# First modulation matrix loaded by feature tile, first two dense units with the contraction outside, small loads on SyncE

## What is computed

```python
x = layer_norm(x, emb_ln_g, emb_ln_b)
cs = jax.nn.silu(c)
mod = cs @ w_ada[l] + b_ada[l]                 # [1, 1024] @ [1024, 6144]
sh1, sc1, gt1, sh2, sc2, gt2 = split(mod, 6)
h = x * (1.0 + sc1) + sh1                      # modulation of the 1024 features
p = h @ w_in[l]                                # then gMLP on one part, RWKV-7 mixing on the other
```

## Time and profile before

| | |
|---|---|
| median of three runs | 1488.13 us (1479.65 to 1488.69) |
| profiled execution | 1484.96 us, its span 1483.1 us |
| PE busy | 1392.3 us, 94% of the span |
| DVE, ACT, POOL busy | 44%, 38%, 33% |
| chain that ended last | PE 82%, DVE 9%, ACT 3%, issue 2%, DMA 2%, POOL 2% |
| PE busy, first two of 40 slices of 37 us | 4 and 8 tenths |

### The profile page before, as it was taken

How to read it: one execution, slowest core, us unless ns; L and a number is a source line. 1 busy time by engine, 2 the same in 40 slices (tenths; PEclk the granted TensorE clock), 3 DMA queues, 4 the chain that set the end, 5 groups by cost and what they waited for, 6 DMA issues and landing times.

```text
span 1483.1 us, 22792 instructions
## 1 busy us (share of the span) xinstructions
PE 1392.3 (94%) x9482; PEld 1146.5 (77%) x9482; DVE 648.0 (44%) x1160; ACT 560.2 (38%) x836; POOL 495.9 (33%) x139
## 2 busy tenths in 40 slices
PE   4899999889899999999997999999999999998998
PEld 1687866775788888878887778888788888887886
DVE  2655677363555333330027524687345444452001
ACT  2435455243432322221214444555454343433122
POOL 1333233014333443433432231112233344443434
PEclk9899999998999999999998998999999999999999
DMA  9662265001312223233212620101221323222221
GB/s 355 188 152 82 86 229 201 31 3 58 113 58 103 96 85 114 85 108 117 88 60 69 249 81 5 58 30 58 72 86 57 114 85 108 92 88 97 96 75 57
DMA packets 24741, 147.93 MB, mean 100 GB/s; under 512 B 2716, under 2 KB 3868, under 8 KB 9024
## 3 DMA queue, kind: packets, MB, share of 16 engines
q1 hardware_dynamic: 19296, 130.96, 24.1%
q10 hardware_dynamic: 5344, 15.51, 3.9%
HBM read 141.74 MB, written 4.72 MB: 99 GB/s over the span
## 4 chain that ended last, share of the span: by engine, by line
PE 82%; DVE 9%; ACT 3%; issue 2%; DMA 2%; POOL 2%; SPq 0%; ACTq 0%; DVEq 0%; POOLq 0%
PE bank L2009 23%; PE bank L2011 22%; PE bank L2010 22%; PE bank L2268 5%; PE bank L1161 2%; DMA raw<-in_weights 2%; POOL weight_lo L1272 2%; PE bank L2175 1%; PE bank L1152 1%; ACT weight_hi L1317 1%; PE bank L1143 1%; DVE bank L1656 1%; PE bank L1070 1%; DVE xres L1656 1%; PE bank L1139 1%
## 5 line engine op out<-in xcount | busy, mean ns | idle before, releaser
L1272 POOL TENSOR_TENSOR weight_lo<-raw,weight_hi 128x2048 fp32r<-128x2048 f32 x98 | 445.7, 4548 | 838.1 <-ACT weight_hi L1317 838.0
L2009 PE MATMUL bank<-act_hi,weight_hi 128*128 128x512 f32 (+1 forms) x1136 | 436.5, 384 | 22.4 <-DVE act_lo L1653 7.1
L2011 PE MATMUL bank<-act_hi,weight_lo 128*128 128x512 f32 (+1 forms) x1136 | 427.3, 376 | 0.0
L2010 PE MATMUL bank<-act_lo,weight_hi 128*128 128x512 f32 (+1 forms) x1136 | 427.1, 376 | 0.0
L1317 ACT ACTIVATE weight_hi<-raw 128x2048 fp32r<-128x2048 f32 x98 | 185.2, 1891 | 403.1 <-PE bank L2011 394.4
L2009 PEld LDWEIGHTS bank<-act_hi,weight_hi 128*128 128x128 f32 x1136 | 218.2, 192 | 63.0 <-issue 15.8
L2011 PEld LDWEIGHTS bank<-act_hi,weight_lo 128*128 128x128 f32 x1136 | 217.7, 192 | 38.9
L2010 PEld LDWEIGHTS bank<-act_lo,weight_hi 128*128 128x128 f32 x1136 | 218.2, 192 | 35.0 <-issue 0.2
L2009 PE MATMUL bank<-weight_hi,hid_hi 128*128 128x512 f32 x352 | 139.0, 395 | 6.9 <-DVE acc L1656 4.7
L2010 PE MATMUL bank<-weight_lo,hid_hi 128*128 128x512 f32 x352 | 138.8, 394 | 0.0
L2011 PE MATMUL bank<-weight_hi,hid_lo 128*128 128x512 f32 x352 | 138.4, 393 | 0.0
(11 more groups left out here) (361 smaller groups left out, 1720.7 us busy)
## 6 DMA issues: line engine op xcount, KB each, us to landing
raw<-in_weights SPq DMA_DIRECT2D x120, 1024.0 KB, 4.6
w<-in_w ACTq DMA_DIRECT2D x2, 2048.0 KB, 10.4
bias_rows<-grow ACTq DMA_DIRECT2D x1, 2560.0 KB
xres<-in_x SPq DMA_DIRECT2D x4, 512.0 KB, 6.7
strip<-bias_rows ACTq DMA_DIRECT2D x1, 2048.0 KB, 9.0
out<-xres SPq DMA_DIRECT2D x3, 512.0 KB, 2.6
row_a<-in_ln_g ACTq DMA_DIRECT2D x2, 512.0 KB, 3.9
row_b<-in_ln_b ACTq DMA_DIRECT2D x2, 512.0 KB, 4.8
```

The lines of the kernel that those rows point to most:

```text
L1272: pool.tensor_tensor(wlo[i % SPLIT][:, :size], raw[n % RAW][:, :size], whi[i % SPLIT][:, :size], ALU.subtract).then_inc(lo_ready, 1)
L2009: pe.matmul(o, l[0], r[0], start=first, stop=False)
L2010: pe.matmul(o, l[0], r[1], start=False, stop=False)
L2011: return pe.matmul(o, l[1], r[0], start=False, stop=last)
```

## The change

- The first 2048 modulation columns are no longer loaded by row tile but by feature tile: `ada0_b` now holds, for feature tile b, all 1024 rows of its 128 sh1 and 128 sc1 columns. The bytes are the same. PE makes eight matmuls of 256 columns (`ada_block`), four at a time in the four column groups of the array, then two matmuls with one column (`columns_block`) that add up the four partial rows by a vector with ones in rows 0, 32, 64, 96 (`group_rows`).
- Every feature tile now has its own chain: `ada_block`, ACT's `mod_half`, `columns_block`, DVE's `mod_column` (three instructions), ACT's `affine_hi`, DVE's `affine_lo`, and the products with it.
- The unit order is now `lora0`, `ada0_0`, `ada0_1`, `k0`, `ada0_2` to `ada0_7`, `lora1`, `k1`, `r0`. Both `lora0` and `k0` run with k outside, interleaved with the modulation blocks; ACT converts `k0` between `affine_hi(0)` and `affine_hi(1)`. `lora1` is third.
- The fifteen small loads go out on SP, after the loads of `ada0_7`, `k1` and `r0`.

```diff
-    win = [("lora0", ((lora, 256),)), ("lora1", ((lora + 160, 128),))]
-    win += [(f"k{j}", ((base + MIX + 256 * j, 256),)) for j in range(2)]
+    win = [("lora0", ((lora, 256),)), ("k0", ((base + MIX, 256),)), ("lora1", ((lora + 160, 128),)),
+           ("k1", ((base + MIX + 256, 256),))]
...
+    first = [(f"ada0_{k}", "w_ada", 0, KC, ((k * P, P), (DM + k * P, P))) for k in range(KC)]
...
-    units = win[:1] + [(f"ada0_{k}", "w_ada", k * P, 1, ((0, 2 * DM),)) for k in range(KC)] + win[1:] + ada
+    units = win[:1] + first[:2] + win[1:2] + first[2:] + win[2:] + ada
...
+    for k in range(KC):
+        b.add(("h1", k), 4 + k % 2, dve=1, act=1)
+        b.add(("ada0", k), 6 + k % 2, act=1, ada=k + 1)
+        b.add(("cols0", k), 6 + k % 2, dve=1)
...
+            elif UNITS[n][0] == "ada0_7":
+                sp.dma_start(relb[0:N_BUCKETS, :], src["rel_bias_t"]).then_inc(load["rel"], 16)
...
+        def mod_half(k):
+
+            await_full(act, ("ada0", k))
+            a.done(act.activation(acc[:, 256 * (k % 2):256 * (k % 2) + 256], bank(("ada0", k))[:, 0:256], ACT.Copy),
+                   drain(("ada0", k), "act"))
+
+        def affine_hi(k):
+
+            await_drained(act, ("cols0", k), "dve")
+            await_full(act, ("h1", k))
+            a.done(act.activation(act_hi[:, k, :], bank(("h1", k))[:], ACT.Identity, bias=affine[:, 1, k:k + 1],
+                                  scale=affine[:, 0, k:k + 1]), drain(("h1", k), "act"))
+
+        for t in range(2):
+            normalise(0, t, S["xn_ready"])
+        mod_half(0)
+        for t in range(2, TT):
+            normalise(0, t, S["xn_ready"])
+        mod_half(1)
+        affine_hi(0)
+        convert()
+        affine_hi(1)
+        for k in range(2, KC):
+            mod_half(k)
+            affine_hi(k)
...
-            if name != W_IN1[-1]:
+            if name not in ("lora1", W_IN1[-1]):
                 convert()
...
+        def mod_column(k):
+
+            b, sh, sc = bank(("cols0", k)), pc[:, COLS["b_sh1"] + k:COLS["b_sh1"] + k + 1], modc[:, k:k + 1]
+            await_full(dve, ("cols0", k))
+            ts(affine[:, 0, k:k + 1], b[:, 257:258], sc, col("emb_g", k), ALU.add, ALU.mult)
+            ts(affine[:, 1, k:k + 1], b[:, 257:258], sc, col("emb_b", k), ALU.add, ALU.mult)
+            stt(affine[:, 1, k:k + 1], b[:, 256:257], sh, affine[:, 1, k:k + 1], ALU.add, ALU.add, sem=drain(("cols0", k), "dve"))
...
+        d.step(V.memset(group_rows, 0.0))
+        for n in range(4):
+            d.step(V.memset(scalars[ROW * n:ROW * n + 1, 0:1], 1.0), S["rows_ready"])
...
+        def ada_block(b):
+
+            n = UNIT_AT[f"ada0_{b}"]
+            claim(pe, ("ada0", b))
+            raw_ready(pe, n)
+            for k in range(KC):
+                r = slice(ROW * (k % 4), ROW * (k % 4) + ROW)
+                mm = pe.matmul(bank(("ada0", b))[r, 0:256], col("c", k).to_broadcast([P, ROW]),
+                               raw[n % RAW][:, 256 * k:256 * k + 256], start=k < 4, stop=k >= 4)
+            mm.then_inc(ada_used, 1)
...
         pe.wait_ge(S["silu_c"], 1)
-        for i in range(5):
-            ada(i)
+        pe.wait_ge(S["rows_ready"], 4)
+        ada_block(0)
+        columns_block(0)
+        ada_block(1)
         pe.wait_ge(load["consts"], 32)
-        turn_x("h1", (S["xn_ready"], 0), features=range(KC - 1))
-        for i in range(5, KC):
-            ada(i)
-        columns(0)
-        turn_x("h1", (S["xn_ready"], 0), features=range(KC - 1, KC))
...
+        turn_x((0, 1), wait=True)
+        columns_block(1)
+        lora0 = next_unit("lora0")
+        for b in range(2, KC):
+            ada_block(b)
+            first_products("lora0", lora0, b - 2)
+            turn_x((b,))
+            columns_block(b)
+            if b == 4:
+                k0 = next_unit("k0")
+            if b >= 4:
+                first_products("k0", k0, b - 4)
+        first_products("lora0", lora0, KC - 2)
+        first_products("k0", k0, KC - 4)
+        first_products("lora0", lora0, KC - 1)
+        for k in range(KC - 3, KC):
+            first_products("k0", k0, k)
```

More of the change, by code:

```diff
@@ L139 @@
 HALF = SEQ // 2
+W_IN1 = ("lora0", "k0", "lora1", "k1", "r0", "r1", "v0", "v1", "pv0", "pv1", "pu0", "pu1")
 class Order:
@@ L2211, in prep_pe @@
+        for k in range(KC - 3, KC):
+            first_products("k0", k0, k)
+        pe.wait_ge(load["rel"], 32)
+        claim(pe, "bias")
+        fill("bias", pe.matmul(bank("bias")[0:N_HEADS, :], relb[0:N_BUCKETS, :], onehot[0:N_BUCKETS, :], start=True, stop=True))
         def prep_pe(p, part):
@@ L2233, in _ @@
             else:
-                dense_feature(name, 1 if name == "lora1" else 2, stage="h1" if name == W_IN1[0] else None)
-            if name == "lora0":
-                pe.wait_ge(load["rel"], 32)
-                claim(pe, "bias")
-                fill("bias", pe.matmul(bank("bias")[0:N_HEADS, :], relb[0:N_BUCKETS, :], onehot[0:N_BUCKETS, :],
-                                       start=True, stop=True))
+                dense_feature(name, 1 if name == "lora1" else 2)
             if name == "r0":
```

142 lines of the change are left out of this document (62 added, 80 removed).

## The result

The changed kernel took 1474.31 us in the median of 20 runs (1466.09 to 1480.44), the kernel before 1481.99 in 20 runs beside them (1472.63 to 1488.81). The ratio is 0.9938, with a 95% interval of 0.9922 to 0.9954: faster by 0.5 to 0.8%, which still counts as "same". The forecast said 1485.3 us, range 1475 to 1492, and same with a chance of 0.92. The direction and the class came out; the number is 11.0 us off, and 0.7 us outside the range.

A forecast was written before the change was run, and what follows sets the result against it. PE, 82% of the last-ending chain, was taken as the bound, so only its idle or slow stretches count. `r0` moves from 86.1 to 83.3 us, 2.8 gained; from the median 1488.13 that gives 1485.3 us, range 1475 to 1492.

The forecast's parts named there:

- The first two blocks: Head: block 0 starts at 13.93 us, its column matmuls end at 18.4, block 1 runs to 20.4.
- The high and low part of `k0`: Head: eight transposes at 0.16 us, high part done at 24.8 us, POOL's low part at 29.5.
- A new wait on SP: `ada0_4`'s load waits for `k0`'s low part; nothing to move from about 25 to 29.5 us, block 4 at 34.1.
- `act_lo(1)`: DVE subtraction held beside POOL's split of `k0`, ending at about 30 us; hidden by the missing block load.
- PE from 34.1 us: Blocks, products and transposes end `k0` at 62.8 us at full clock, 64.0 with 1.2 us for slow clock.
- What is late next: Ahead of `r0`: tile 1's row pair, held by POOL, delays the low-rank inputs about 1.3 us; `r0` at 83.3 us.
- The shift of `r0`: End of the head: `r0` starts at 83.3 us instead of 86.1, the whole gain of 2.8 us.
- The small loads: Fifteen loads moved from ACT to SP: priced at nothing, as their 4.61 us are covered on either engine.
- Rival 1: Head: no hole in the loads, `r0` at about 78.0 us, gain 8 us, 1480 us; chance 0.14.
- Rival 2: PE at 1.2 GHz from 22 to 62 us: `r0` at 105, 19 us slower, 1507 us; chance 0.04 in full.
- rival 3: Head's seams cost 0.3 us instead of 0.1: `r0` 2 us later, 1490 us; chance 0.25 with partly slow clock.
- My last test: If `r0` starts as forecast but the total moves by over 5 us otherwise, the only-the-head-matters reading is wrong.

The follow-up runs named there:

- the row edit: Changed kernel with DVE's row pair of token tile 1 moved behind the shift of `lora1`; cut after `pu1` 189.7 us against 190.9, whole 1476.3 against 1474.9.
- the first pair: The first profiled executions of the whole kernel before and the whole changed kernel: 1484.96 and 1477.79 us.
- the cut kernels: Kernels stopped behind the unit `pu1`, everything after it left out: before 194.6 us, changed 190.9 us.
- the pause filled: Kernel before plus four unread matmuls in PE's pause ahead of the first product; cut after `pu1` 192.6 us against 194.6, whole 1478.8 against 1482.3.
- the kernel with `k0` later: Changed kernel, stopped behind `pu1`, with `k0`'s load and conversion two blocks later: 189.7 us against 190.9.
- both edits: Changed kernel with `k0` loaded and converted two blocks later and tile 1's row pair behind `lora1`'s shift; whole 1471.5 us against 1474.9, cut after `pu1` 187.9 against 190.9.

## Why the prediction was right or wrong

By its own steps:

- *The first two blocks.* Block 0 came at 14.40 and not 13.93 (the load landed later by itself), its column at 18.12 (forecast 17.8). Right within 0.4 us.
- *The high and low part of `k0`.* Its transposes took 1.97 us where I had 8 x 0.16 = 1.3: the 0.16 came from a stretch in which PE was mostly at full pace, and these ran at the slower one (blocks of 1.93 us on both sides, where later ones take 1.07). The low part ended at 29.98, forecast 29.5.
- *A new wait on SP.* As forecast: issue at 30.0 (29.5), no transfer from 26 to 28 us, block 4 at 34.94 (34.1), a wait of 1.72 us (1.7).
- *`act_lo(1)`.* As the rows beside POOL before: 2.68 us, ending 0.55 us after POOL, forecast "about 30"; it ended at 30.53. The later ones, 2.95 and 3.53 us, ended 0.5 and 1.1 us after POOL as well. The Trainium skill, "SBUF — State Buffer", section "Who interferes with whom", says that the later instruction of such a pair is held until the earlier is through; these three agree.
- *PE from 34.1 us.* The last matmul of `k0` started at 62.25, forecast end 64.0. The work was right: 62.8 had been the number at full clock, from 34.1, and with block 4 at 34.94 it took 27.7 us instead of 28.7. The 1.2 us for the clock was not needed in this execution; two others lost 1.8 us there, three none. As a mean of the two ends it was a fair price.
- *What is late next.* Forecast `r0` at 83.3, with the row pair of tile 1 as the cause: 82.2, mean of five 82.8, and the row edit took 1.2 us away. Right.
- *The shift of `r0`.* 2.8 us forecast, 3.9 in the first pair, 2.8 in the mean of eight profiled executions, 3.6 by the times of the cut kernels. The heads of before among the eight start `r0` anywhere from 84.8 to 86.1 us, so that it is 2.8 to the tenth is luck.
- *The small loads.* Priced at nothing. Cut they cost nothing that can be seen, but whole, alone, they cost 3.1 us (0.2 to 6.0). Whether they cost anything within the change was not tested.

Two steps failed. The one is the sentence "from `r0` on both kernels have the same order, so the whole effect is the shift of that start". The order is the same, but the time is not: it depends on where half-clock stretches fall, and the kernel before has 83.6 us of them in an execution, of which I saw and priced one, 5 us long and worth 2.4. With the change it is 19.2 us less, and by the relation between runs that goes with the whole gain of 7.4 us; how much of this the clock causes is not shown by an experiment. I had the right rows, the 0.50 at 40 to 42 us, and used them for the new head only, as a possible loss, never for the old one as a loss that it has on average in more places than the profile shows.

The other is "against the median I predict": three runs with a spread of 9 us were taken for the level. The median of 20 lies 6.1 us lower, and the profiled execution, which I had held to be 3.2 us under the level, was 2.7 over the mean of 90. The sum against that mean would have been 1479.5.

Rival 1 had the right size (a gain of 8) by the wrong mechanism: the hole in the loads was there, and `r0` was never near 78. Rival 2, the slow clock throughout, is refuted; rival 3's seams cost no more than I had charged. My last test was a total that moves by more than 5 us otherwise than `r0`. It was not met: 7.7 less 3.9 us is 3.8 in the first pair, 7.4 less 2.8 is 4.6 in the means. Set that wide, it missed what the cut kernels show, 3.8 us (1.9 either way) beyond the first 190 us. So the reading that only the head matters fell short all the same.

## What to carry to other kernels

Before a small gain is priced from one profile, read the granted clock over the whole span and the runs' own spread. Where some 80 us of an execution are at the half clock, as here, an edit that closes pauses on PE may be worth more than the idle time it saves, and a small gain can vanish in the spread; compare kernels at equal half-clock time as well.

A product that needs a converted operand should not have its conversion queued behind the buffer of the unit just running: here there was a wait for `k0` in every version in which it stood behind `lora1`, of 2.5 to 2.9 us (1.4 with the pause filled). And a POOL split beside DVE's two-input operations wants to be put where DVE has slack: the hole in the loads and the held `act_lo` were two places of one cost, and filling the hole moved the wait, 1.94 us for 1.72.

## What the runs showed of the hardware

The mean granted clock differs from execution to execution of one kernel, from 0.966 to 0.980 for the whole kernel before, and with it the time from 1489 to 1471 us. The places differ too: in three profiled executions of the old head, up to 50 us, the half clock was at about 36 to 47 us only, at 22 to 29 and 39 to 46, and at 24 to 30 and 37 to 44.

The record reads 1.00 in the first 20 us although blocks take 1.94 us there where later ones take 1.07, so a start at the slower pace does not show in the granted clock of a row; the durations do.

Waits of about the same length were not always followed by the half clock. Ahead of `k0`, those of 2.46 and 2.47 us were not, three times out of three, and of four of 2.91 to 2.94 us three were. At block 4, those of 1.77 and 1.62 us were, and those of 1.72, 1.71 and 1.61 us were not. The 1.94 us wait of the kernel with `k0` later was, and the two of 1.95 us in the whole kernel with both edits were not.
